# Dense feed-forward of a two-layer trunk: gate and up by seven half-size block products

## The chip, the cores and the metric

The kernel runs on one core of one Trainium2 chip. The metric is device time in microseconds (us), the median of several runs. Five engines work side by side and meet at semaphores: PE (TensorE) multiplies matrices, DVE (VectorE), ACT (ScalarE) and POOL (GpSimd) work on elements, SP (SyncE) issues the loads.

## What is computed

Two residual layers over 512 tokens of width 1024. The first has a mixer (gated convolution and a state-space scan) and then a dense SwiGLU; the second has differential attention and a mixture of 8 experts. The change concerns the dense SwiGLU, whose hidden width is 2816 = 22 tiles of 128:

```python
def swiglu(x, w_gate, w_up, w_down):
    return (jax.nn.silu(x @ w_gate) * (x @ w_up)) @ w_down

x = x + swiglu(rmsnorm(x, even_norm_ffn[i]), ffn_w_gate[i], ffn_w_up[i], ffn_w_down[i])
```

## The kernel before

Every product of float32 matrices is made of three passes. A matrix is split into a high part (rounded to TensorE's fp32r format) and a low part (the rest), and high x high, high x low and low x high are summed in PSUM. Activations are split once; weights are split as they arrive.

**Weight units.** `units` (L280 to L292) lists all weights of the trunk in the order of use, 512 KB each: `feature_unit` is 128 output features for all 1024 inputs, 8 blocks of 128 x 128; `token_unit` is 2 blocks of 128 inputs by 512 outputs. SP loads unit u into one of `RAW_SLOTS` = 4 slots of `raw` once POOL is through with unit u - 4 (`load`, L358). ACT rounds it into `w_hi` (`high_parts`, L993), one of `HL_SLOTS` = 4 slots, once TensorE has used unit u - 4 (`unit_used`). POOL subtracts, `w_lo = raw - w_hi` (`low_parts`, L1293, instruction L1305), and counts `lo_done`, for which TensorE waits in `begin_unit`. Each engine goes through its list in the order written by hand.

**Feed-forward.** The 22 hidden tiles come in two halves of 11 (`HALF_FT`), each followed by its part of the down projection (`token_out`, L430), which is added to the residual stream. A hidden tile n is two units, gate and up. `feature_out` (L419) makes one: 24 matmuls with 128 x 128 of weights held still and 512 tokens moving, into one PSUM bank:

```python
for k in range(KD):
    wh, wl = w_hi[:, s, k * P:(k + 1) * P], w_lo[:, s, k * P:(k + 1) * P]
    pe.matmul(ps[:, bank, :], wh, xh[:, k, :], start=(k == 0), stop=False)
    pe.matmul(ps[:, bank, :], wh, xl[:, k, :], start=False, stop=False)
    last = pe.matmul(ps[:, bank, :], wl, xh[:, k, :], start=False, stop=(k == KD - 1))
```

The first two tiles are made by `first_features` (L505) in two token halves of 256, because tokens 256 to 511 are still being normalized and turned then. Around a tile, ACT takes silu of the gate (L1151), DVE multiplies by the up bank (L1699, `ff_val`), ACT rounds the result (L1156, `ff_hi`), and POOL subtracts (L1381, `ff_lo`). `htmp` is a scratch tile of the normalization; `act_a_hi` and `act_a_lo` are the split activations, with features on partitions; `act_b_hi` and `act_b_lo` are free in this stage.

Of the kernel before, what the change touches and what calls it, by code (L numbers as in the profile page):

```python
# [16 lines left out]
F32 = mybir.dt.float32  # L17
# [4 lines left out]
ALU = mybir.AluOpType  # L22
# [64 lines left out]
FF_HALF = 2 * HALF_FT + 2 * HALF_UNITS  # L87
U_QKV = U_FF + 2 * FF_HALF
# [17 lines left out]
def build_trunk(nc, t, h_slots):  # L106
# [68 lines left out]

    q_tok, o = place("q_tok", [P, NT, D], F32, scratch)
# [105 lines left out]
    units = [feature_unit(w_in, COL_XBC + P * f) for f in range(XBC_TILES)]  # L282
    units += [token_unit(w_in, 2 * k, COL_Z + 512 * g) for g in range(2) for k in range(4)]
    units += [feature_unit(w_in, c + P * a) for a in range(KD) for c in (COL_CG, COL_HV, 0)]
    units += [token_unit(w_out, 2 * k, 512 * g) for g in range(2) for k in range(8)]
    for half in range(2):
        units += [feature_unit(w, P * f) for f in range(half * HALF_FT, (half + 1) * HALF_FT)
                  for w in (w_gate, w_up)]
        units += [token_unit(w_down, half * HALF_FT + 2 * k, 512 * g, min(2, HALF_FT - 2 * k))
                  for g in range(2) for k in range(HALF_UNITS)]  # L290
    units += [token_unit(w_qkv, 2 * k, 512 * g) for g in range(6) for k in range(4)]
    units += [token_unit(w_o, 2 * k, 512 * g) for g in range(2) for k in range(4)]  # L292
    assert len(units) == N_UNITS

    def size(u):
        return units[u][1][0] * units[u][1][1]
# [49 lines left out]
    def _(sp):  # L346
# [11 lines left out]
        def load(u):  # L358
            src, (k, n) = units[u]
            if u >= RAW_SLOTS:  # L360
                sp.wait_ge(lo_done, u - RAW_SLOTS + 1)
            sp.dma_start(raw[:, u % RAW_SLOTS, 0:k * n].rearrange("p (k n) -> p k n", k=k),
                         src).then_inc(unit_in[u % RAW_SLOTS], 16)
# [6 lines left out]
        for u in range(N_UNITS):  # L370
# [31 lines left out]
            if u == U_FF + 2 * FF_HALF - 6:  # L402
# [12 lines left out]
    def _(pe):  # L415
# [3 lines left out]
        def feature_out(u, bank, xh, xl):  # L419
# [8 lines left out]
            last.then_inc(unit_used, 1)  # L428

# [393 lines left out]
        for half in range(2):  # L823
            u0 = U_FF + half * FF_HALF
            if half:
                pe.wait_ge(acc_evac, 12)
            else:
                first_features(2, u0, lambda i: pe.wait_ge(acc_evac, 5 + i))
            for f in range(0 if half else 2, HALF_FT):
                n = half * HALF_FT + f  # L830
                pe.wait_ge(ff_mul, n - 1)
                feature_out(u0 + 2 * f, HID_BANK[half] + 2 * (n % 2), act_a_hi, act_a_lo)
                feature_out(u0 + 2 * f + 1, HID_BANK[half] + 2 * (n % 2) + 1, act_a_hi, act_a_lo)
            if half:
                pe.wait_ge(acc_evac, 16)
# [154 lines left out]
    def _(act):  # L990
        made = [0]

        def high_parts(upto):  # L993

            while made[0] <= min(upto, N_UNITS - 1):
                u = made[0]
                act.wait_ge(unit_in[u % RAW_SLOTS], 16 * (u // RAW_SLOTS + 1))
                if u >= HL_SLOTS:
                    act.wait_ge(unit_used, u - HL_SLOTS + 1)
                act.activation(w_hi[:, u % HL_SLOTS, 0:size(u)], raw[:, u % RAW_SLOTS, 0:size(u)],  # L1000
                               ACT.Copy).then_inc(hi_done, 1)
# [142 lines left out]
        for half in range(2):  # L1144
            u0 = U_FF + half * FF_HALF
            for f in range(HALF_FT):
                n = half * HALF_FT + f
                after(u0 + 2 * f)
                if n >= 2:
                    act.wait_ge(ff_mul, n - 1)  # L1150
                act.activation(ff_gate[:, n % 2, :], ps[:, HID_BANK[half] + 2 * (n % 2), :], ACT.Silu).then_inc(ff_silu, 1)  # L1151
                high_parts(u0 + 2 * f + 1 + AHEAD)
                act.wait_ge(ff_mul, n + 1)
                if half and f == 0:
                    act.wait_ge(unit_used, u0)
                act.activation(ff_hi[:, f, :], ff_val[:, n % 2, :], ACT.Copy).then_inc(ff_hi_done, 1)  # L1156
            high_parts(min(u0 + FF_HALF - 1 + AHEAD, U_QKV - 1))

# [251 lines left out]
    def _(dve):  # L1410
# [280 lines left out]
        for half in range(2):  # L1691
            u0 = U_FF + half * FF_HALF
            for f in range(HALF_FT):
# [3 lines left out]
                if n >= 2:  # L1697
                    dve.wait_ge(ff_lo_done, n - 1)
# [1289 lines left out]
```

## Time and profile before

| | |
|---|---|
| median of 3 runs | 1919.18 us (1919.08 to 1919.76) |
| the profiled execution, first to last instruction | 1917.3 us |
| TensorE busy | 1898.1 us, 99% of the span |
| DVE, ACT, POOL busy | 806.7, 717.9, 550.5 us |
| mean granted TensorE clock | 0.999 of full |
| feed-forward, gate and up of the first tile to the down projection's end | about 369 to 731 us |

The profile is of one execution; its span leaves out the start and the end of the program, and the median lies 1.9 us above it. Times within it count from the span's start. Matmuls overlap, so the step from one start to the next is what a matmul costs, and not its recorded duration. A DVE, ACT or POOL instruction's duration includes whatever it waited for after it was issued.

### The profile page before, as it was taken

Reading aid. Unit: us, or ns where it says so; the run is one execution under the profiler, and the core shown is the slowest. Engines: PE = TensorE matmul, PEld = TensorE weight load, DVE = VectorE, ACT = ScalarE, POOL = GpSimd, SP = SyncE. Lnnn points to the kernel's source line nnn. Section 1 sums busy time; section 2 is a strip of 40 time slices with the busy share of each in tenths; the row PEclk is TensorE's granted clock in tenths of the full one; section 3 lists DMA queues with packets and bytes.
Section 4 is the critical chain, followed back from the end, with each engine's and each line's share of the span. In section 5 each row is a group of like instructions: output and inputs, shape, how many; then the busy total and the mean of one; then the engine's idle time right before and its main releaser. Section 6 shows DMA issues by size and latency. Waiting matters only on the chain.

```text
span 1917.3 us, 29421 instructions
## 1 busy us (share of the span) xinstructions
PE 1898.1 (99%) x11978; PEld 1641.2 (86%) x11978; DVE 806.7 (42%) x1240; ACT 717.9 (37%) x1124; POOL 550.5 (29%) x332
## 2 busy tenths in 40 slices
PE   9999999999999999999999999999999999999998
PEld 7888788888888887877679999999999877888886
DVE  6465552200000006866741110100101776999996
ACT  5332232332222224367640001000000655878785
POOL 4466664365445544432321002010010100200000
PEclk9999999999999999999999999999999999999999
DMA  9523223233233332311119989888888787999993
GB/s 351 177 77 99 67 99 99 77 110 99 91 107 88 94 112 77 100 47 43 56 34 399 372 311 341 290 296 300 304 300 305 273 284 264 411 407 391 371 396 145
DMA packets 283561, 396.21 MB, mean 207 GB/s; under 512 B 12736, under 2 KB 190912, under 8 KB 283424
## 3 DMA queue, kind: packets, MB, share of 16 engines
q1 hardware_dynamic: 279488, 381.67, 56.7%
q0 software_dynamic: 3936, 12.62, 1.7%
q8 instruction: 97, 1.59, 0.3%
q14 instruction: 40, 0.33, 0.1%
HBM read 374.48 MB, written 21.08 MB: 206 GB/s over the span
## 4 chain that ended last, share of the span: by engine, by line
PE 96%; ACT 1%; DVE 1%; issue 1%; DMA 0%; DVEq 0%; POOL 0%; ACTq 0%; POOLq 0%; SPq 0%
PE ps L2200 17%; PE ps L2207 8%; PE ps L2264 6%; PE ps L2266 6%; PE ps L2265 6%; PE ps L425 6%; PE ps L427 6%; PE ps L426 6%; PE ps L443 3%; PE ps L445 3%; PE ps L444 3%; PE ps L572 2%; PE ps L574 2%; PE ps L573 2%; PE ps L462 1%; PE ps L460 1%
## 5 line engine op out<-in xcount | busy, mean ns | idle before, releaser
L1305 POOL TENSOR_TENSOR w_lo<-raw,w_hi 128x1024 fp32r<-128x1024 f32 (+2 forms) x193 | 386.9, 2021 | 346.9 <-ACT w_hi L1000 346.8
L2051 DVE TENSOR_TENSOR s_lo<-s_raw,s_hi 128x1024 fp32r<-128x1024 f32 x264 | 318.7, 1246 | 43.8 <-ACT s_hi L2461 36.3
L2461 ACT ACTIVATE s_hi<-s_raw 128x1024 fp32r<-128x1024 f32 x264 | 272.9, 1060 | 70.1 <-PE ps L2266 46.3
L1000 ACT ACTIVATE w_hi<-raw 128x1024 fp32r<-128x1024 f32 x158 | 163.4, 1043 | 188.0 <-PE ps L445 115.6
L2803 DVE TENSOR_TENSOR hid<-ps,silu_g 128x160 f32<-128x160 f32 x88 | 28.6, 325 | 409.9 <-ACT silu_g L2421 409.8
L425 PE MATMUL ps<-act_a_hi,w_hi 128*128 128x512 f32 x512 | 199.6, 390 | 0.0
L426 PE MATMUL ps<-act_a_lo,w_hi 128*128 128x512 f32 x512 | 199.3, 389 | 0.0
L427 PE MATMUL ps<-act_a_hi,w_lo 128*128 128x512 f32 x512 | 199.2, 389 | 0.0
L2584 POOL TENSOR_TENSOR sum_rows<-sum_rows,y_rows_sb 128x1024 f32<-128x1024 f32 (+1 forms) x12 | 28.6, 2380 | 580.1 <-ACT y_rows_sb L2426 320.4
L2421 ACT ACTIVATE silu_g<-ps 128x160 f32<-128x160 f32 x88 | 26.8, 304 | 447.6 <-PE ps L2200 447.6
L2200 PE MATMUL ps<-xT,w_gate 128*128 128x132 f32 x1408 | 172.9, 276 | 0.4 <-DMA w_up<-in_moe_w_up 0.4
L2200 PE MATMUL ps<-xT,w_up 128*128 128x132 f32 x1408 | 172.8, 276 | 0.0
L2200 PEld LDWEIGHTS ps<-xT,w_gate 128*128 128x128 f32 x1408 | 165.2, 190 | 0.6 <-issue 0.6
L2207 PE MATMUL ps<-hid,w_down 128*128 128x132 f32 x1408 | 165.4, 276 | 0.0
L2200 PEld LDWEIGHTS ps<-xT,w_up 128*128 128x128 f32 x1408 | 165.2, 190 | 0.0
L2207 PEld LDWEIGHTS ps<-hid,w_down 128*128 128x128 f32 x1408 | 161.5, 190 | 0.2
L2264 PE MATMUL ps<-s_hi,s_x_hi 128*128 128x512 f32 (+1 forms) x384 | 145.5, 379 | 0.0
L2266 PE MATMUL ps<-s_hi,s_x_lo 128*128 128x512 f32 (+1 forms) x384 | 142.9, 372 | 0.0
L2265 PE MATMUL ps<-s_lo,s_x_hi 128*128 128x512 f32 (+1 forms) x384 | 142.7, 372 | 0.0
L425 PEld LDWEIGHTS ps<-act_a_hi,w_hi 128*128 128x128 f32 x512 | 96.1, 188 | 22.3 <-issue 2.4
L427 PEld LDWEIGHTS ps<-act_a_hi,w_lo 128*128 128x128 f32 x512 | 96.1, 188 | 20.2
L426 PEld LDWEIGHTS ps<-act_a_lo,w_hi 128*128 128x128 f32 x512 | 96.1, 188 | 19.9
(464 smaller groups left out, 3158.4 us busy)
## 6 DMA issues: line engine op xcount, KB each, us to landing
w_gate<-in_moe_w_gate SPq DMA_DIRECT2D x44, 1024.0 KB, 5.3
w_up<-in_moe_w_up SPq DMA_DIRECT2D x44, 1024.0 KB, 8.5
w_down<-in_moe_w_down SPq DMA_DIRECT2D x44, 1024.0 KB, 10.5
s_raw<-in_moe_w_gate SPq DMA_DIRECT2D x44, 1024.0 KB, 8.3
s_raw<-in_moe_w_up SPq DMA_DIRECT2D x44, 1024.0 KB, 8.3
s_raw<-in_moe_w_down SPq DMA_DIRECT2D x44, 1024.0 KB, 8.0
raw<-in_even_w_in SPq DMA_DIRECT2D x42, 512.0 KB, 3.8
raw<-in_attn_w_qkv SPq DMA_DIRECT2D x24, 512.0 KB, 3.7
```

The lines of the kernel that those rows point to most:

```text
L425: pe.matmul(ps[:, bank, :], wh, xh[:, k, :], start=(k == 0), stop=False)
L426: pe.matmul(ps[:, bank, :], wh, xl[:, k, :], start=False, stop=False)
L427: last = pe.matmul(ps[:, bank, :], wl, xh[:, k, :], start=False, stop=(k == KD - 1))
L1000: act.activation(w_hi[:, u % HL_SLOTS, 0:size(u)], raw[:, u % RAW_SLOTS, 0:size(u)], ACT.Copy).then_inc(hi_done, 1)
L1305: ins = pool.tensor_tensor(w_lo[:, u % HL_SLOTS, cut], raw[:, u % RAW_SLOTS, cut], flat(w_hi[:, u % HL_SLOTS, cut]), ALU.subtract)
L2051: return eng.tensor_tensor(s_lo[u % S_HL][:], s_raw[u // 2 % S_RAW][:, u % 2, :], s_hi[u % S_HL][:].bitcast(F32), ALU.subtract)
L2200: mm = pe.matmul(ps[:, bank, i * CAP:i * CAP + width], w_slots[s][i][:, k, c:c + P], xT[:, k, 0:width], start=(k == 0), stop=(k == KD - 1))
L2207: mm = pe.matmul(ps[:, d // 3, (d % 3) * CAP:(d % 3) * CAP + width], w_slots[s][2][:, f % 2, d * P:(d + 1) * P], hid[:, f, 0:width], start ...
L2264: pe.matmul(out, sh, wh, start=first, stop=False, skip_group_check=True)
L2265: pe.matmul(out, sh, wl, start=False, stop=False, skip_group_check=True)
L2266: return pe.matmul(out, sl, wh, start=False, stop=last, skip_group_check=True)
L2461: act.activation(s_hi[u % S_HL][:], s_raw[q % S_RAW][:, u % 2, :], ACT.Copy).then_inc(s_high, 1)
```

## The change

Tiles 0 and 1 stay as they were. For each of the other 20 tiles the kernel takes gate and up as one product of blocks. The inputs (k) are cut in two halves of 512, the tokens in two halves of 256, and the outputs are gate and up, so that each of four results (gate or up, tokens low or high) was the sum of two block products, eight in all. A scheme of the Strassen-Winograd kind makes the four results of seven block products, on sums of blocks:

- **Weights.** DVE makes four sums of weight blocks for each tile, 512 wide: t1 and t4 in `w_sums_b`, t2 and t3 in `w_sums_a`, which is `htmp` (`weight_sums`). A tile is now four units (`paired`): the gate as loaded, `w_sums_a`, `w_sums_b`, and half of the up as loaded. ACT rounds and POOL subtracts 3.5 x 1024 columns a tile where it was 2 x 1024. Loads are a list of their own (`loads`, `freed_by`).
- **Activations.** Four sums of activation blocks, 1024 wide, are made once: `h_feat` is the unsplit activation (ACT copies it from PSUM for tokens 256 to 511, POOL adds high and low parts for tokens 0 to 255), DVE makes the sums, ACT rounds them to `act_b_hi`, DVE subtracts to `act_b_lo`.
- **Products.** `paired_out` makes the seven products, 12 matmuls of 256 columns each. Partial results are kept in SBUF: ACT copies the first (`part_1`); DVE adds (`part_16`, `part_167`, and four more sums). `part_kept` and `part_read` tell TensorE that a bank may be written again.
- **Hidden tile.** Silu is taken in two halves; the second waits for `late_gate`. The product of gate and up now has both inputs in SBUF. The low part `ff_lo` moves from POOL to DVE (`low_hidden`).

```diff
+        def paired_out(n):
+            u0, b, m = pair_unit(n), pair_bank(n), n - PLAIN_F
...
+            def product(bank, u, at, source, first):
+                s = u % HL_SLOTS
+                for k in range(4):
+                    xh, xl = source(k)
+                    c = at + k * P
+                    wh, wl = w_hi[:, s, c:c + P], w_lo[:, s, c:c + P]
+                    pe.matmul(ps[:, bank, 0:256], wh, xh, start=(first and k == 0), stop=False, skip_group_check=True)
+                    pe.matmul(ps[:, bank, 0:256], wh, xl, start=False, stop=False, skip_group_check=True)
+                    last = pe.matmul(ps[:, bank, 0:256], wl, xh, start=False, stop=(k == 3), skip_group_check=True)
+                return last
+
+            first_pair = n == PLAIN_F
+            begin_unit(u0)
+            if n != PLAIN_F + 1:
+                pe.wait_ge(ff_mul, n - 1)
+            product(b, u0, 0, from_tile(0, 0), True).then_inc(part_done, 1)
+            begin_unit(u0 + 1)
...
+            product(b + 1, u0 + 1, 0, from_sum(1), True).then_inc(part_done, 1)
+            pe.wait_ge(part_kept, m + 1)
+            product(b, u0, 512, from_tile(4, 0), False).then_inc(unit_used, 1)
...
+            product(b + 2, u0 + 1, 512, from_sum(2), True).then_inc(unit_used, 1)
+            begin_unit(u0 + 2)
...
+            product(b + 3, u0 + 2, 0, from_sum(0), True).then_inc(part_done, 1)
+            pe.wait_ge(part_read, 2 * m + 1)
+            product(b + 2, u0 + 2, 512, from_tile(4, 256), False).then_inc(unit_used, 1)
+            begin_unit(u0 + 3)
...
+            pe.wait_ge(part_read, 2 * m + 2)
+            product(b + 3, u0 + 3, 0, from_sum(3), False).then_inc(unit_used, 1)
...
+        for n in range(PLAIN_F, FT):
+            u0, b, m = pair_unit(n), pair_bank(n), n - PLAIN_F
+            act.wait_ge(part_done, 3 * m + 1)
...
+            act.activation(part_1[:], ps[:, b, 0:256], ACT.Copy).then_inc(part_kept, 1)
+            if n != HALF_FT:
+                high_hidden(n - 1)
+            act.wait_ge(unit_used, u0 + 1)
+            act.activation(ff_gate[:, n % 2, 0:256], ps[:, b, 0:256], ACT.Silu).then_inc(ff_silu, 1)
+            high_parts(u0 + 5)
+            act.wait_ge(late_gate, m + 1)
+            act.activation(ff_gate[:, n % 2, 256:512], part_1[:], ACT.Silu).then_inc(ff_silu, 1)
+            high_parts(u0 + 7)
...
+        low_parts(U_FF + 1)
+        for tt in (0, 1):
+            cut = slice(tt * P, (tt + 1) * P)
+            pool.wait_ge(lo_ev, 8 + 2 * tt + 2)
+            pool.tensor_tensor(h_feat[:, :, cut], flat(act_a_hi[:, :, cut]), flat(act_a_lo[:, :, cut]), ALU.add
+                               ).then_inc(h_kept, 1)
         low_parts(U_WO - 1)
...
+        def weight_sums(n):
...
+            if m:
+                dve.wait_ge(lo_done, pair_unit(n - 1) + 3)
+            dve.tensor_tensor(t1, b12, b11, ALU.subtract)
+            dve.tensor_tensor(t3, b22, b12, ALU.subtract)
+            dve.drain()
+            dve.tensor_tensor(t2, b22, t1, ALU.subtract)
+            dve.drain().then_inc(w_sums_made, 1)
+            dve.tensor_tensor(t4, b21, t2, ALU.subtract).then_inc(w_sums_made, 1)
...
+            dve.tensor_tensor(part_16[:], ps[:, b + 1, 0:256], part_1[:], ALU.add)
+            if n + 1 < FT and n + 1 != HALF_FT:
+                weight_sums(n + 1)
+            dve.wait_ge(unit_used, u0 + 2)
+            dve.drain()
+            dve.tensor_tensor(part_167[:], ps[:, b + 2, 0:256], part_16[:], ALU.add).then_inc(part_read, 1)
```

How DVE's list changes: before, these two rows were all that DVE did for the 11 tiles of the first half (`ps` is PSUM, `x9` counts repeats):

```order
L1699 TENSOR_TENSOR ff_val_88<-ps,ff_gate_87 128x512 [waits ff_silu,unit_used] x2
L1699 TENSOR_TENSOR ff_val_88<-ps,ff_gate_87 128x512 [waits ff_lo_done,ff_silu,unit_used] x9
```

Now DVE has these rows for one paired tile, here tile 2, with the weight sums of tile 3 in it (the line numbers are of the changed file):

```order
L1896 TENSOR_TENSOR part_16_91<-ps,part_1_90 128x256 [waits part_kept,part_done]
L1853 TENSOR_TENSOR w_sums_b_89<-raw_54 128x512 [waits lo_done,unit_in1,unit_in0]
L1854 TENSOR_TENSOR htmp_58<-raw_54 128x512
L1856 TENSOR_TENSOR htmp_58<-raw_54,w_sums_b_89 128x512
L1858 TENSOR_TENSOR w_sums_b_89<-raw_54,htmp_58 128x512
L1901 TENSOR_TENSOR part_167_92<-ps,part_16_91 128x256 [waits unit_used]
L1904 TENSOR_TENSOR ff_val_88<-ps,part_167_92 128x256 [waits part_done]
L1906 TENSOR_TENSOR part_1_90<-ps,part_16_91 128x256 [waits unit_used]
L1908 TENSOR_TENSOR ff_val_88<-ps,part_16_91 128x256 [waits unit_used]
L1911 TENSOR_TENSOR ff_val_88<-ff_val_88,ff_gate_87 128x512 [waits ff_silu]
L1868 TENSOR_TENSOR ff_lo_86<-ff_val_88,ff_hi_85 128x512 [waits ff_hi_done]
```

One instruction a tile has become eleven; six of them, L1853 to L1858, L1911 and L1868, read nothing from `ps`. The sum `part_167`, for which TensorE's sixth product waits, stands behind the four weight sums of the next tile.

POOL's list where the feed-forward begins; before (the 18 are units up to the fifth of the feed-forward):

```order
L1305 TENSOR_TENSOR w_lo_56<-raw_54,w_hi_55 128x1024 [waits hi_done] x18
L1381 TENSOR_TENSOR ff_lo_86<-ff_val_88,ff_hi_85 128x512 [waits ff_hi_done]
L1305 TENSOR_TENSOR w_lo_56<-raw_54,w_hi_55 128x1024 [waits hi_done] x2
```

and now (the 15 are units up to its second):

```order
L1458 TENSOR_TENSOR w_lo_56<-raw_54,w_hi_55 128x1024 [waits hi_done] x15
L1531 TENSOR_TENSOR h_feat_93<-act_a_hi_50,act_a_lo_51 128x8x128 [waits lo_ev] x2
L1458 TENSOR_TENSOR w_lo_56<-raw_54,w_hi_55 128x1024 [waits hi_done] x3
L1458 TENSOR_TENSOR w_lo_56<-htmp_58,w_hi_55 128x1024 [waits hi_done]
L1458 TENSOR_TENSOR w_lo_56<-w_sums_b_89,w_hi_55 128x1024 [waits hi_done]
L1458 TENSOR_TENSOR w_lo_56<-raw_54,w_hi_55 128x512 [waits hi_done]
```

The two additions stand ahead of the third unit of the feed-forward, and each paired tile has three subtractions of 1024 and one of 512 in a row.

## Rows read from the trace of the kernel before

**Rows 1.** the page: engines, the chain that ended last, weight loads.
```profile
PE 1898.1 (99%) x11978; PEld 1641.2 (86%) x11978; DVE 806.7 (42%) x1240; ACT 717.9 (37%) x1124; POOL 550.5 (29%) x332
...
PE 96%; ACT 1%; DVE 1%; issue 1%; DMA 0%; DVEq 0%; POOL 0%; ACTq 0%; POOLq 0%; SPq 0%
...
L425 PEld LDWEIGHTS ps<-act_a_hi,w_hi 128*128 128x128 f32 x512 | 96.1, 188 | 22.3 <-issue 2.4
```

**Rows 2.** busy time by stretch, feed-forward; behind POOL the granted clock, DMA share, GB/s.
```profile
395.00:440.00 45.00, 45.00 (x200) 37.28 (x199) 2.77 (x4) 13.60 (x18) 25.79 (x14) 1.00 0.39 115
```

**Rows 3.** timeline of TensorE, 512 columns: start us, duration us, engine, line, operation.
```profile
393.58 0.40 PE L425 MATMUL ps<-act_a_hi,w_hi 128*128 128x512 f32 x1
...
404.49 0.39 PE L425 MATMUL ps<-act_a_hi,w_hi 128*128 128x512 f32 x1
...
415.37 0.39 PE L425 MATMUL ps<-act_a_hi,w_hi 128*128 128x512 f32 x1
```

**Rows 4.** the list of waits, TensorE's longest: us in total, times, longest us.
```profile
PE ps L668 <- POOLq L1317: 2.3, 1, 2.3
```

**Rows 5.** timeline of TensorE, 256 columns.
```profile
376.23 0.36 PE L518 MATMUL ps<-act_a_hi,w_hi 128*128 128x256 f32 x1
...
382.06 0.28 PE L518 MATMUL ps<-act_a_hi,w_hi 128*128 128x256 f32 x1
...
393.22 0.28 PE L518 MATMUL ps<-act_a_hi,w_hi 128*128 128x256 f32 x1
```

**Rows 6.** timeline of ACT beside the third tile.
```profile
399.74 1.05 ACT L1000 ACTIVATE w_hi<-raw 128x1024 fp32r<-128x1024 f32 x1
405.42 0.63 ACT L1156 ACTIVATE ff_hi<-ff_val 128x512 fp32r<-128x512 f32 x1 [4.62 <-DVE ff_val L1699]
```

**Rows 7.** timeline of POOL: four units, the third of the feed-forward, the third tile.
```profile
300.64 9.46 POOL L1305 TENSOR_TENSOR w_lo<-raw,w_hi 128x1024 fp32r<-128x1024 f32 x4 [16.32 <-ACT w_hi L1000]
...
370.98 3.40 POOL L1305 TENSOR_TENSOR w_lo<-raw,w_hi 128x1024 fp32r<-128x1024 f32 x1
...
400.87 2.39 POOL L1305 TENSOR_TENSOR w_lo<-raw,w_hi 128x1024 fp32r<-128x1024 f32 x1 [1.79 <-ACT w_hi L1000]
406.12 1.29 POOL L1381 TENSOR_TENSOR ff_lo<-ff_val,ff_hi 128x512 fp32r<-128x512 f32 x1 [2.86 <-ACT ff_hi L1156]
```

**Rows 8.** timeline of DVE beside the third tile.
```profile
404.69 0.69 DVE L1699 TENSOR_TENSOR ff_val<-ps,ff_gate 128x512 f32<-128x512 f32 x1 [10.21 <-PE ps L427]
```

**Rows 9.** instruction groups by form, 256 wide, on DVE and on ACT: busy us, mean ns.
```profile
L1746 DVE TENSOR_TENSOR htmp<-ps,rot_s 128x256 f32<-128x256 f32 x16 | 6.6, 413 | 0.0
...
L1203 ACT ACTIVATE probs<-ps,soft 128x256 f32<-128x256 f32 x16 | 7.4, 464 | 1.9 <-DVE soft L1764 1.9
```

**Rows 10.** DMA issues: count, KB each, us to landing.
```profile
raw<-in_ffn_w_gate SPq DMA_DIRECT2D x22, 512.0 KB, 3.7
```

**Rows 11.** timeline of DVE where POOL is busy too.
```profile
133.82 2.10 DVE L1611 SCALAR_TENSOR_TENSOR mix<-mix,cbm 128x512 f32<-128x512 f32 x1
135.85 1.52 DVE L1611 SCALAR_TENSOR_TENSOR mix<-mix,cbm 128x512 f32<-128x512 f32 x1
...
756.39 0.68 DVE L1745 TENSOR_TENSOR htmp<-ps,rot_c 128x512 f32<-128x512 f32 x1
...
757.83 0.69 DVE L1751 TENSOR_TENSOR htmp<-htmp 128x512 f32<-128x512 f32 x1
...
758.71 2.63 DVE L1755 TENSOR_TENSOR q_tok<-htmp,head_ss 128x512 f32<-128x512 f32 x1
```

**Rows 12.** timeline of POOL in the same stretches, one instruction a row.
```profile
133.47 1.91 POOL L1333 TENSOR_TENSOR xdt<-xs,dts 128x1024 f32<-128x1024 f32 x1
135.33 1.50 POOL L1346 TENSOR_TENSOR spans<-act_b_lo,dts 128x512 fp32r<-128x512 f32 x1
...
755.35 2.42 POOL L1305 TENSOR_TENSOR w_lo<-raw,w_hi 128x1024 fp32r<-128x1024 f32 x1 [13.09 <-ACT w_hi L1000]
757.84 2.94 POOL L1305 TENSOR_TENSOR w_lo<-raw,w_hi 128x1024 fp32r<-128x1024 f32 x1
```

More of the change, by code:

```diff
@@ L291, in build_trunk, with plain, paired @@
-    units += [token_unit(w_qkv, 2 * k, 512 * g) for g in range(6) for k in range(4)]
-    units += [token_unit(w_o, 2 * k, 512 * g) for g in range(2) for k in range(4)]
+    loads, units, freed_by = [], [], []
+    def plain(parts):
+        for src, shape in parts:
+            units.append(("raw", len(loads), 0, shape[0] * shape[1]))
+            freed_by.append(len(units))
+            loads.append((src, shape))
+    def paired(gate, up):
+        r, u = len(loads), len(units)
+        loads.extend((gate, up))
+        freed_by.extend((u + 3, u + 4))
+        units.extend((("raw", r, 0, UNIT), ("sums_a", 0, 0, UNIT), ("sums_b", 0, 0, UNIT), ("raw", r + 1, UNIT // 2, UNIT // 2)))
@@ L293, in build_trunk, with whole, wait_whole @@
+    plain(token_unit(w_qkv, 2 * k, 512 * g) for g in range(6) for k in range(4))
+    plain(token_unit(w_o, 2 * k, 512 * g) for g in range(2) for k in range(4))
     assert len(units) == N_UNITS
     def size(u):
-        return units[u][1][0] * units[u][1][1]
+        return units[u][3]
+    def whole(u):
+        home, r, at, n = units[u]
+        tile = {"raw": raw[:, r % RAW_SLOTS, :], "sums_a": w_sums_a, "sums_b": w_sums_b}[home]
+        return tile[:, at:at + n]
+    def wait_whole(eng, u):
+        home, r, at, n = units[u]
+        if home == "raw":
+            eng.wait_ge(unit_in[r % RAW_SLOTS], 16 * (r // RAW_SLOTS + 1))
+        else:
+            half = u >= U_PAIRS[1]
+            m = (u - U_PAIRS[half]) // PAIR_UNITS + (HALF_FT - PLAIN_F if half else 0)
+            eng.wait_ge(w_sums_made, 2 * m + (1 if home == "sums_a" else 2))
@@ L369, in _ @@
         zero_blocks = range(0, h_slots.shape[0], P)
-        for u in range(N_UNITS):
+        for u in range(len(loads)):
             load(u)
@@ L401, in _ @@
                 load_gain(3)
[L402 removed]
+            if u == units[U_QKV - 6][1]:
                 sp.wait_ge(ff_lo_done, FT)
@@ L827, in _ @@
             else:
[L828 to L835, printed above, removed]
+                first_features(2, U_FF, lambda i: pe.wait_ge(acc_evac, 5 + i))
+            for n in range(HALF_FT if half else PLAIN_F, HALF_FT * (half + 1)):
+                if n == HALF_FT + 1:
+                    pe.wait_ge(acc_evac, 16)
+                paired_out(n)
             def hidden_tiles(i, tt):
@@ L1143, in _ @@
         norm_by_tile(1, 2, U_FF, lambda tt: act.wait_ge(acc_evac, 5 + tt))
[L1144 to L1157, printed above, removed]
+        for tt in (2, 3):
+            for half in range(2):
+                act.wait_ge(lo_ev, 8 + 2 * tt + half + 1)
+                act.activation(h_feat[:, 4 * half:4 * half + 4, tt * P:(tt + 1) * P],
+                               ps[:, TURN_BANK[2] + (2 * tt + half) % 4, :].rearrange("p (a b) -> p a b", a=4), ACT.Copy
+                               ).then_inc(h_kept, 1)
```

203 lines of the change are left out of this document (150 added, 53 removed).

## The prediction, made before the changed kernel was run

> **What bounds the kernel now.** I read the page first: TensorE is busy 99% of the span, and it makes up 96% of the chain that ended last [rows 1]. So a saving has to shorten TensorE's own work, and whatever makes it wait is paid in full. Then the busy times by stretch, for the feed-forward [rows 2]: in 45 us TensorE has no gap at full granted clock (1.00, the 2.4 GHz level), POOL is busy 25.8 us and DVE 2.8. POOL, not DVE, is the engine with work there. Then the timelines. A hidden tile n (gate and up) begins every 10.9 us [rows 3]: 48 matmuls of 512 columns at 0.2267 us. The list of waits has nothing over 2.3 us on TensorE [rows 4].
>
> **The matmuls.** Matmuls of 256 columns already run in the first two tiles: from 382.06 to 393.22 there are 93 starts, 0.120 us each [rows 5]. A paired tile has 7 products of 12, 84 x 0.120 = 10.08 us, against 10.88. That is 0.80 less, 16.1 us for 20 tiles: less than the eighth that the count of columns promises (1.36 a tile), since a matmul costs some 13 ns beside its columns at both sizes. This is all the change can gain.
>
> **What it adds to the others, per paired tile.** ACT rounds four weight units (three of 1024, one of 512) where it had two, 1.05 us for 1024 [rows 6]. POOL subtracts the same four: 3 x 2.36 + 1.25 = 8.33 us, from four in a row in 9.46 us, single ones being recorded at 2.39 and 1.29 [rows 7]; its 1.29 us low part of the hidden tile goes to DVE. DVE had one instruction of 0.69 us [rows 8]; now it has four weight sums of 512, five sums of 256 out of PSUM at 0.41 [rows 9], the product and the low part: some 5.5 us back to back. Loads are as many as before, two of 512 KB a tile, each landed 3.7 us after its issue [rows 10]; their raw slots come free with POOL's third and fourth unit, and they land some 5 us ahead of their weight sums. I cost them at nothing; if POOL's units slip over 5 us more, they are next.
>
> **The port between DVE and POOL.** This decides. At 757.83 DVE begins a tensor_tensor with both inputs in SBUF, and the POOL unit that begins at 757.84 takes 2.94 us instead of 2.39. At 758.71 DVE asks for another one: it takes 2.63 instead of 0.69 and ends 0.56 us after that POOL unit [rows 11, 12]. Between engines that both have work they alternate, one instruction each: at 133.82 two DVE instructions in a row take 2.10 and 1.52 us, each ending 0.54 after a POOL instruction [rows 11, 12]. With one input in PSUM there is no such wait: 0.68 us at 756.39, in the middle of a POOL unit of 2.42 [rows 11, 12]. Of DVE's new instructions, six have both inputs in SBUF: the four weight sums, the product of ff_val and ff_gate, and the low part. Before, no DVE instruction of these tiles did. The port then needs 8.33 + 6 x 0.54 = 11.6 us a tile, already over 10.88.
>
> **The loop that sets the pace.** TensorE's sixth product waits for part_read, which DVE gives after the next tile's weight sums. Without the port: the second product ends 3.1 us into the tile; product and low part of the tile before are done by 3.2; part_16 at 3.6, four weight sums with two drains by 6.3, part_167 at 6.8. It is needed at 7.2 less 0.24 (a weight load of 0.19 [rows 1] and a hop of 0.05, estimated): 0.15 us to spare, where one port wait is up to 2.4. With the port, from the start of a sixth product: it and its tail 1.64; DVE part_1 0.42 (2.1); ACT's late silu, 256 wide, 0.3 (2.4; the nearest row, a 256 wide exponential, has 0.46 [rows 9]); ACT rounds the third unit of the next tile (3.5); POOL subtracts it, and the product waits behind it (5.9); product 0.69 (6.5); ACT rounds the hidden tile 0.63 (7.2); DVE's low part waits behind POOL's fourth unit and ends at 8.3; part_16 and the first weight sum (9.1); POOL has meanwhile taken its turn with the first unit of the tile after, and the second weight sum waits for it, to 12.1; third and fourth with their drains 13.7; part_167 14.2; TensorE goes on at **14.4**. That is 10.08 of work and a stall of 4.3 us ahead of each sixth product. Every step is a row or a sum of rows; the ends are small: hops of 0.02 or 0.08, POOL 5% faster or slower and a hop to TensorE of 0.1 or 0.35 move it from 13.8 to 14.7.
>
> It holds for the tiles that have a late tile before them and a weight sum behind: not for n = 10 and 21, which make no sums for a next tile, nor for n = 11, which begins after the down projection with all its units ready. Tile 2 comes as late, since its low parts wait on the sums of activations. 17 x (14.4 - 10.88) = +59.8 us; 3 x (10.08 - 10.88) = -2.4.
>
> **The first two tiles.** POOL now adds two tiles of h_feat ahead of its third weight unit. Before, that unit ran from 370.98 to 374.38 [rows 7], and TensorE took it at 376.23 [rows 5]. The adds are 2.4 us each (the size of a unit; at least 1.9, as the 1024 wide row at 133.47 [rows 12]), so the unit ends at 379.1: **+3.0** (+2 to +3.5). The other sums of activations on DVE and ACT, about 5 us and 4 us, lie beside the 11.5 us of the second token half. Behind the last tile nothing moves.
>
> **Sum**: +59.8 - 2.4 + 3.0 = +60.4. On the profiled span of 1917.3 that is 1977.7; the runs' median is 1.9 above that span, so **1979.6 us**, said as 1980. A measurement of this kernel can tell about 0.2%, 3.8 us, from no change.
>
> **Rivals.**
> - *A clock that falls.* Before, TensorE never waits over 2.3 us [rows 4] and its clock reads 1.00. Now it would stand for 4.3 us of every 14.4. If the clock goes to its 1.2 GHz level there, the sixth product takes up to 1.43 us more, and it is in the loop (the seventh is mostly not: the product waits for POOL anyway): 17 x 1.43 = +24, 2004 us. No row speaks for or against, as no such gap is in the trace; the stretch at work between two gaps, 10 us, speaks against a lasting fall. Chance 0.17. The Trainium skill (TensorE: Matmul & The Clock Gate, HAM oscillation) says that a kernel with waits between bursts falls to half rate at each wait and has to earn the clock again; by that rule the time would be this rival's, and no run here shows it yet.
> - *The port packs well.* If DVE and POOL fill it without holes, a tile costs the port's 11.6 us: 17 x 0.7 - 2.4 + 3.0 = +12.5, about 1932 us. For it: the port's sum is a floor. Against it: the loop above is a chain of waits in a fixed order, with the port empty in two places of it (while DVE sums out of PSUM and while ACT rounds). It decides if the third unit reaches POOL before DVE's last sum. Anything between this and the forecast is possible. Chance 0.10. The Trainium skill (SBUF — State Buffer, SBUF: two separate sides) has the pair of ports locked by whoever starts first for the whole instruction, not shared by bandwidth; sharing would bring the time toward this rival, and the rows at 757.83 and 758.71 side with the lock.
> - *Faster after all.* If two SBUF inputs cost DVE no wait on these tiles, or under 0.15 us, the tile is 10.08: -16.1 + 3.0 = -13.1, 1906 us. Its place is the sixth product's wait, its price 0.80 us a tile gained. Against it stand six port waits a tile. Chance 0.05.
> - *That the change doesn't do what it says* can be left out: the listing of its instructions has 84 matmuls of 256 columns for a paired tile.
>
> **How the numbers follow.** Forecast 0.68, with 1965 to 1992 as its own range. The clock 0.17, packing 0.10, faster 0.05. The range must leave out no more than 2 in 10: from 1945 (packing in part) to 2010 (the clock). Faster 0.05, within 0.2% 0.01, slower 0.94.
>
> **What would show it.** Right: in the timeline, tiles 3 to 9 and 13 to 20 begin 14.4 us apart, 10 and 11 10.1 apart; TensorE waits 4 us for DVE's part_167, 17 times; DVE's second weight sum is recorded at 2.5 to 3 us, the product at over 2.5; POOL's units stay under 3. Weight sums of 0.69 us beside a busy POOL would make the loop wrong; matmuls of 0.21 us behind the stall would show the clock; tiles at 11.6 the packing. If the first weight sum waits instead of the second, the time is the same within 0.3 us a tile.

## The result, and the profile after

The changed kernel takes **1990.38 us** (median of 4 runs, 1990.19 to 1990.86) against 1919.22 of the kernel before (4 runs): a ratio of 1.0372, with a 95% interval of 1.0357 to 1.0387. It is slower, as forecast, and the time lies 10.4 us above the 1980 of the prediction, inside its range. The profiled execution's span went from 1917.3 to 1988.5 us, +71.2.

The page of the changed kernel: engines, granted clock of TensorE by slice, chain that ended last.

```profile
PE 1916.1 (96%) x12698; PEld 1693.1 (85%) x12698; DVE 1004.8 (51%) x1450; ACT 768.2 (39%) x1212; POOL 621.9 (31%) x352
...
PEclk9999999988999889999999999999999999999999
...
PE 86%; DVE 7%; ACT 2%; POOL 1%; DVEq 1%; issue 1%; DMA 0%; ACTq 0%; POOLq 0%; SPq 0%
```

TensorE went from 96% of the chain [rows 1] to 86%, and DVE from 1% to 7%. TensorE's busy time did not fall but rose by 18 us, although the paired tiles have fewer columns. Slower matmuls are in it: the granted clock falls below nine tenths only in slices of the feed-forward, and by their starts the slow matmuls of the paired tiles take 26 us more than they would at full pace. The list of waits of the changed kernel (us in total, times, longest) names the new ones:

```profile
PE ps L519 <- DVE part L1901: 50.9, 17, 5.2
PE ps L639 <- POOL w_lo L1458: 2.6, 1, 2.6
```

L1901 makes `part_167`, and L519 begins the sixth product. The second row is the prologue, which is what I call the stretch ahead of the first paired tile. By stretch, in the changed kernel (busy us of PE, PEld, DVE, ACT, POOL, then granted clock, DMA share, GB/s):

```profile
395.00:440.00 45.00, 34.95 (x255) 34.34 (x253) 34.00 (x34) 18.88 (x28) 27.66 (x13) 0.85 0.28 83
```

Against [rows 2], DVE is busy 34.0 us where it had 2.8, POOL hardly more (27.7 against 25.8), and the clock is 0.85 in place of 1.00. More than a third of DVE's 34 us is waiting inside instructions: in this stretch and with the times that each form takes alone (0.42, 0.69 and, for 1024 columns, 1.23 us in e7), its instructions would take some 22 us (an estimate). One tile shows the waits. DVE in the changed kernel (start, us, line, operands):

```profile
431.78 1.79 DVE L1911 TENSOR_TENSOR ff_val<-ff_val,ff_gate 128x512 f32<-128x512 f32 x1
434.27 1.01 DVE L1868 TENSOR_TENSOR ff_lo<-ff_val,ff_hi 128x512 fp32r<-128x512 f32 x1 [0.70 <-ACT ff_hi L1278]
...
435.54 0.68 DVE L1853 TENSOR_TENSOR w_sums_b<-raw 128x512 f32<-128x512 f32 x1
436.13 0.68 DVE L1854 TENSOR_TENSOR htmp<-raw 128x512 f32<-128x512 f32 x1
436.89 0.69 DVE L1856 TENSOR_TENSOR htmp<-raw,w_sums_b 128x512 f32<-128x512 f32 x1
437.70 2.66 DVE L1858 TENSOR_TENSOR w_sums_b<-raw,htmp 128x512 f32<-128x512 f32 x1
440.45 0.42 DVE L1901 TENSOR_TENSOR part<-ps,part 128x256 f32<-128x256 f32 x1
```

and POOL beside it:

```profile
430.62 2.40 POOL L1458 TENSOR_TENSOR w_lo<-w_sums_b,w_hi 128x1024 fp32r<-128x1024 f32 x1 [2.68 <-ACT w_hi L1117]
432.98 1.75 POOL L1458 TENSOR_TENSOR w_lo<-raw,w_hi 128x512 fp32r<-128x512 f32 x1
437.04 2.76 POOL L1458 TENSOR_TENSOR w_lo<-raw,w_hi 128x1024 fp32r<-128x1024 f32 x1 [2.32 <-ACT w_hi L1117]
439.76 2.82 POOL L1458 TENSOR_TENSOR w_lo<-htmp,w_hi 128x1024 fp32r<-128x1024 f32 x1
```

The product ends 0.55 us behind POOL's unit (433.57 against 433.02), the low part 0.55 behind the next (435.28 against 434.73), the fourth weight sum 0.56 behind the one after (440.36 against 439.80): the pattern of [rows 11, 12], three times in a tile. TensorE in the changed kernel, around its stalls:

```profile
425.75 0.58 PE L519 MATMUL ps<-act_a_hi,w_hi 128*128 128x256 f32 x1 [3.31 <-DVE part L1901]
...
426.56 0.41 PE L519 MATMUL ps<-act_a_hi,w_hi 128*128 128x256 f32 x1
426.78 0.41 PE L520 MATMUL ps<-act_a_lo,w_hi 128*128 128x256 f32 x1
...
438.20 0.28 PE L521 MATMUL ps<-act_b_hi,w_lo 128*128 128x256 f32 x1
440.93 0.39 PE L519 MATMUL ps<-act_a_hi,w_hi 128*128 128x256 f32 x1 [2.45 <-DVE part L1901]
```

Behind this stall the matmuls start 0.21 us apart where they need 0.12: the lower of the two clock levels, for one product or two. The fall doesn't always come at once. In tile 6 the sixth product begins at 470.88 at the full pace and slows down near its end; ten of the seventeen tiles have such a delay:

```profile
471.94 0.28 PE L521 MATMUL ps<-act_a_hi,w_lo 128*128 128x256 f32 x1
472.06 0.32 PE L519 MATMUL ps<-act_a_hi,w_hi 128*128 128x256 f32 x1
472.18 0.41 PE L520 MATMUL ps<-act_a_lo,w_hi 128*128 128x256 f32 x1
472.39 0.42 PE L521 MATMUL ps<-act_a_hi,w_lo 128*128 128x256 f32 x1
```

Behind the stall of tile 12, 3.6 us long, no matmul is slow. From all starts in this trace: tiles 2 to 9 and 12 to 20 take between 13.6 and 17.1 us, 14.89 on the mean, against 10.88 before; 10, 11 and 21 take 10.1 to 10.3. The first pair starts at 397.96 in place of 393.58 [rows 3]. So 17 x (14.89 - 10.88) = +68.2, three tiles -2.1, prologue +4.4: +70.5 of the span's +71.2.

### The profile page after: what moved, and what is told of

Same layout as the page of the kernel before. It is cut to its first block, busy times and chain, and to the rows that moved or that the text cites. A ratio compares the mean times of both kernels' runs of the same rounds, so it can differ in the third digit from the quotient of the medians.

```text
span 1988.5 us, 31362 instructions
## 1 busy us (share of the span) xinstructions
PE 1916.1 (96%) x12698; PEld 1693.1 (85%) x12698; DVE 1004.8 (51%) x1450; ACT 768.2 (39%) x1212; POOL 621.9 (31%) x352
## 4 chain that ended last, share of the span: by engine, by line
PE 86%; DVE 7%; ACT 2%; POOL 1%; DVEq 1%; issue 1%; DMA 0%; ACTq 0%; POOLq 0%; SPq 0%
PE ps L2413 16%; PE ps L2420 8%; PE ps L2477 6%; PE ps L2479 6%; PE ps L2478 6%; PE ps L564 3%; PE ps L565 3%; PE ps L566 3%; PE ps L495 2%; PE ps L496 2%; PE ps L497 2%; PE ps L693 2%; PE ps L519 2%; PE ps L695 2%; PE ps L694 2%; PE ps L521 2%
## 5 line engine op out<-in xcount | busy, mean ns | idle before, releaser
L1458 POOL TENSOR_TENSOR w_lo<-raw,w_hi 128x1024 fp32r<-128x1024 f32 (+2 forms) x193 | 377.6, 1974 | 337.2 <-ACT w_hi L1117 337.0
L1117 ACT ACTIVATE w_hi<-raw 128x1024 fp32r<-128x1024 f32 (+1 forms) x158 | 154.9, 990 | 185.4 <-PE ps L566 103.4
L519 PE MATMUL ps<-act_a_hi,w_hi 128*128 128x256 f32 x240 | 76.0, 317 | 50.9 <-DVE part L1901 50.9
L519 PEld LDWEIGHTS ps<-act_a_hi,w_hi 128*128 128x128 f32 x240 | 51.7, 216 | 54.4 <-DVE part L1901 54.3
L519 PE MATMUL ps<-act_b_hi,w_hi 128*128 128x256 f32 x320 | 97.6, 305 | 0.0
L520 PE MATMUL ps<-act_b_lo,w_hi 128*128 128x256 f32 x320 | 97.1, 303 | 0.0
L521 PE MATMUL ps<-act_b_hi,w_lo 128*128 128x256 f32 x320 | 96.7, 302 | 0.0
L2477 PEld LDWEIGHTS ps<-s_hi,s_x_hi 128*128 128x128 f32 x384 | 72.3, 188 | 14.1 <-issue 1.6
## 6 DMA issues: line engine op xcount, KB each, us to landing
w_down<-in_moe_w_down SPq DMA_DIRECT2D x44, 1024.0 KB, 10.3
```

Source lines behind the costliest of these rows:

```text
L519: pe.matmul(ps[:, bank, 0:256], wh, xh, start=(first and k == 0), stop=False, skip_group_check=True)
L520: pe.matmul(ps[:, bank, 0:256], wh, xl, start=False, stop=False, skip_group_check=True)
L521: last = pe.matmul(ps[:, bank, 0:256], wl, xh, start=False, stop=(k == 3), skip_group_check=True)
L1117: act.activation(w_hi[:, u % HL_SLOTS, 0:size(u)], whole(u), ACT.Copy).then_inc(hi_done, 1)
L1458: ins = pool.tensor_tensor(w_lo[:, u % HL_SLOTS, cut], whole(u)[:, cut], flat(w_hi[:, u % HL_SLOTS, cut]), ALU.subtract)
L2477: pe.matmul(out, sh, wh, start=first, stop=False, skip_group_check=True)
```

## The experiments

Runs that were made together share runs of the kernel before: its median is 1921.29 for e1 to e4, 1919.27 for e5 to e7, 1919.16 for e8 and e9. Ratios are to those.

**e1_no_port: is it the port?** For the tiles from 3 on (tile 11 left out), each weight sum reads a bank of PSUM that TensorE is through with in place of one of its two blocks, and the hidden product stays in PSUM, so no DVE instruction of the loop has two inputs in SBUF. ACT and POOL round and subtract the raw block for the two summed units. Instructions are as many. The weight sums and all that follows from them have other values; the experts then get other numbers of rows, so that the whole time (one run, 2613.48 us, span 2611.7) means nothing and only the feed-forward is read.

```diff
...
-            dve.tensor_tensor(t1, b12, b11, ALU.subtract)
...
+            there = ps[:, pair_bank(n - 1) + 1, :] if n not in (PLAIN_F, HALF_FT) else None
+            for out, one, two, then in ((t1, b12, b11, 0), (t3, b22, b12, 2), (t2, b22, t1, 3), (t4, b21, t2, 1)):
...
+                    ins = dve.tensor_tensor(out, there, two, ALU.subtract)
...
```

> DVE's instructions stay as many and as long, but none of the paired tiles' reads two inputs in SBUF: the weight sums read a PSUM bank in place of one block (so the sums are wrong, and the rounding takes the gate's block instead; all that follows is computed on wrong values), and the hidden product is held in PSUM. If waits for the port between DVE and POOL make the loop: tiles 3 to 9 and 13 to 20 begin 10.1 us apart instead of 14.8, TensorE's wait for part_167 is gone, the granted clock is 1.00, and the down projection ends about 80 us earlier. If it is DVE's own work and its order: tiles stay over 13 us and the wait stays. The expert layer gets other values and perhaps other routing, so only the stretch up to the down projection's end is compared.

Measured: every tile from 4 on takes 10.08 us (tile 3: 10.24), and only tile 2 waits for `part_167`. The window behind it, same columns as above:

```profile
440.00:480.00 40.00, 40.00 (x336) 40.00 (x335) 23.81 (x44) 20.30 (x32) 33.72 (x16) 1.00 0.36 103
```

The timeline of e1 shows DVE's hidden product, its low part and the first weight sum inside four POOL units in a row, which end at 429.19, and the second weight sum across their end, each at its own length:

```profile
420.71 8.48 POOL L1462 TENSOR_TENSOR w_lo<-raw,w_hi 128x1024 fp32r<-128x1024 f32 x4 [2.85 <-ACT w_hi L1117]
```
```profile
425.57 0.70 DVE L1925 TENSOR_TENSOR ps<-ps,ff_gate 128x512 f32<-128x512 f32 x1
427.41 0.69 DVE L1881 TENSOR_TENSOR ff_lo<-ps,ff_hi 128x512 fp32r<-128x512 f32 x1 [1.14 <-ACT ff_hi L1281]
...
428.35 0.68 DVE L1862 TENSOR_TENSOR w_sums_b<-ps,raw 128x512 f32<-128x512 f32 x1
428.94 0.68 DVE L1862 TENSOR_TENSOR htmp<-ps,raw 128x512 f32<-128x512 f32 x1
```

Same engines, same chain of waits, same count of work; with one input moved to PSUM the loss is gone, all of it. It is the port, and the gain of 0.80 us a tile was real. The last paired matmul starts at 666.0, 75 us ahead of the changed kernel.

**e2_val_in_psum: two port instructions fewer.** The hidden product is held in PSUM (L1911 and L1868 then have one input there); the weight sums stay.

```diff
...
+                dve.tensor_tensor(ff_lo[:, f, :], ps[:, pair_bank(n) + 1, :],
+                                  flat(ff_hi[:, f, :]), ALU.subtract).then_inc(ff_lo_done, 1)
...
-            dve.tensor_tensor(ff_val[:, n % 2, :], ff_val[:, n % 2, :], ff_gate[:, n % 2, :], ALU.mult).then_inc(ff_mul, 1)
+            dve.tensor_tensor(ps[:, b + 1, :], ps[:, b + 1, :], ff_gate[:, n % 2, :], ALU.mult).then_inc(ff_mul, 1)
...
```

> Only the hidden product and its low part lose their second SBUF input (the values are held in a PSUM bank that TensorE has finished with); the weight sums keep theirs. Waiting for whole POOL instructions: the product no longer waits for a POOL unit, tiles 12.8 to 13.1 us apart, 1960 us (1955 to 1967). If only the sum of port times counted (0.54 us for each of the two): 1972. If the clock alone made the difference: no change, 1990.

1958.19 us (1955.13 to 1960.16), 1.0189 (1.0172 to 1.0206): nearly half of the loss comes back. The total is as expected, the tiles are not: they do not take 13 us each but, from tile 5 on and with few exceptions, in turn 14.2 and 10.1. In the long ones the fourth weight sum takes 2.65 us, in the short ones 0.69. My reading, which no run tests, is that the wait in one tile shifts DVE against POOL so that the sums of the next are clear of its units. The long tiles hold slow matmuls too: 14.2 us is 10.1 of work, a stall 2.6 longer than a step, and 1.5 of lower clock.

```profile
PE ps L519 <- DVE part L1909: 30.8, 12, 5.2
```

**e3_pool_in_pieces: the same instructions on DVE, POOL's in pieces.** POOL's subtractions in the feed-forward are cut to 256 columns.

```diff
-                step = 256 if u >= U_QKV + 20 else 1024
+                step = 256 if u >= U_QKV + 20 or U_PAIRS[0] <= u < U_DOWN[0] or U_PAIRS[1] <= u < U_DOWN[1] else 1024
```

> POOL's subtractions of the paired tiles in pieces of 256 columns instead of 1024, everything else as in the change. If DVE waits for the POOL instruction that holds the port, whatever its length, it now waits 0.66 us at most: tiles about 12.8 to 13.3 us apart, 1963 us (1956 to 1972), though POOL is busy longer (0.66 us a piece, 9.2 us a tile for 8.3). If it is POOL's total work that counts: slower, 2003.

1965.76 us (1964.99 to 1967.04), 1.023 (1.0213 to 1.0248). A DVE instruction now waits for one piece only. DVE in e3, a second and a third weight sum:

```profile
432.26 1.22 DVE L1854 TENSOR_TENSOR htmp<-raw 128x512 f32<-128x512 f32 x1
433.56 1.07 DVE L1856 TENSOR_TENSOR htmp<-raw,w_sums_b 128x512 f32<-128x512 f32 x1
```

So the waits have the length of POOL's instruction, not of its work; but now every sum pays some 0.4 us, where one in four paid 2.0. The four together still wait 1.7 us a tile; the hidden product, at 0.69 to 1.26 us in place of 1.77 to 2.92, gained more.

**e4_fill_the_stall: does the clock cost anything?** Twenty-two idle matmuls of 128 columns run in each stall, their output never read. They write a bank that DVE has read for the tile before, so TensorE first waits for that tile's product (`ff_mul`), which is done by then.

```diff
+            if n not in (HALF_FT - 1, HALF_FT, FT - 1):
+                pe.wait_ge(ff_mul, n)
+            for _ in range(0 if n in (HALF_FT - 1, HALF_FT, FT - 1) else 22):
+                pe.matmul(ps[:, pair_bank(n - 1) + 1, 0:P], ones[:], t_incl[:], start=True, stop=True, skip_group_check=True)
             pe.wait_ge(part_read, 2 * m + 1)
```

> 22 matmuls of 128 columns without use (some 2.2 us) between TensorE's fifth and sixth product, where it stands still for 2.4 to 4 us; no engine waits for them. If the fall of the clock costs what rows of the change show (sixth and seventh product at up to 0.229 us a matmul): granted clock back to 1.00, all matmuls at 0.120, tiles 14.4 us apart, 1983 us (1979 to 1986). If the slow matmuls lie beside DVE's and POOL's loop: clock back, time the same within 2 us.

1993.27 us (1992.6 to 1994.0), 1.0376 (1.0359 to 1.0394), no different from the changed kernel; clock 1.00, tiles of 14.99 (tile 2: 15.56). It looks as if the clock were free, but the trace says otherwise. TensorE in e4, where `part_167` had ended at 438.21:

```profile
434.27 5.08 PE L546 MATMUL ps<-t_incl,ones 128*128 128x128 f32 x44
439.10 0.36 PE L519 MATMUL ps<-act_a_hi,w_hi 128*128 128x256 f32 x1
```

An idle matmul shows as two records 0.112 us apart, so that the 22 last 5 us, where I had taken 2.2; together they outlast the stall: the sixth product begins 0.89 us behind `part_167`, where without them it follows 0.06 behind (440.93 after 440.87 in the changed kernel). That is 0.8 us a tile. This run fills too much and proves nothing; e8 does it again.

**e8_shorter_fill.** The same with 16.

```diff
-            for _ in range(0 if n in (HALF_FT - 1, HALF_FT, FT - 1) else 22):
+            for _ in range(0 if n in (HALF_FT - 1, HALF_FT, FT - 1) else 16):
```

> The same filling of the stall with 16 idle matmuls in place of 22. In the run with 22 the idle matmuls lasted from 434.27 to 439.35, while part_167 had ended at 438.21: the filling itself held the sixth product back by some 0.65 us, 17 times, so that run could not show what the lower clock costs. Sixteen take 3.6 us of a stall of 3.9 and end before part_167. If the lower clock behind a stall is on the path: tiles of 14.3 to 14.4 us where the changed kernel has 14.9 on the mean, 17 x 0.5 = 9 less, some 1981 us, ratio 1.0325 (1.031 to 1.034). If the lower clock costs nothing: tiles of 14.9, ratio 1.037 as the changed kernel.

**1977.38 us** (five runs 1976.49 to 1978.32; one more took 1995.32, at a mean granted clock of 0.947, for a reason that the record doesn't show), 1.032 (1.0291 to 1.0348), below the changed kernel's interval: the lower clock costs the changed kernel 13 us. The tiles take 14.17 us each, without spread but for tile 2 (15.56) and tile 12 (13.67), 14.22 on the mean. The twelve matmuls of the sixth product, from the first start to the first of the seventh, take 26.1 us over the 17 tiles, where the changed kernel has 37.1; these 11.0 us are nearly all of the 11.4 by which the 17 tiles differ. TensorE and DVE in e8:

```profile
435.68 3.74 PE L546 MATMUL ps<-t_incl,ones 128*128 128x128 f32 x32
439.67 0.39 PE L519 MATMUL ps<-act_a_hi,w_hi 128*128 128x256 f32 x1 [0.26 <-DVE part L1905]
```
```profile
429.18 2.92 DVE L1915 TENSOR_TENSOR ff_val<-ff_val,ff_gate 128x512 f32<-128x512 f32 x1
432.79 1.01 DVE L1872 TENSOR_TENSOR ff_lo<-ff_val,ff_hi 128x512 fp32r<-128x512 f32 x1 [0.70 <-ACT ff_hi L1282]
...
434.66 2.87 DVE L1858 TENSOR_TENSOR htmp<-raw 128x512 f32<-128x512 f32 x1
...
439.19 0.42 DVE L1905 TENSOR_TENSOR part<-ps,part 128x256 f32<-128x256 f32 x1
```

With the clock held this is the forecast's loop, step by step. The sixth product began at 425.49 (one tile before 439.67); from there the product ends at 6.6 (forecast 6.5), the low part at 8.3 (8.3), the second weight sum, which is the one that waits, at 12.0 (12.1), `part_167` at 14.1 (14.2).

**e5_h_feat_later: the prologue.** POOL adds h_feat behind the third and fourth weight unit, not ahead of them.

```diff
-        low_parts(U_FF + 1)
+        low_parts(U_FF + 3)
```

> Only the order of POOL in the first tiles: the two additions of h_feat behind the fourth weight unit instead of behind the second. TensorE's wait of 2.6 us for the third unit goes; if nothing else takes its place the time is 2.5 us less than that of the change (3.7% above the kernel before becomes 3.6%). If the sums of activations then come later and tile 2 waits for them, the gain is given back at tile 2, and the time is that of the change within 1 us.

1989.55 us (1987.34 to 1990.03), 1.0363 (1.0345 to 1.038). The 2.6 us wait at L639 is gone and the first pair starts at 394.70, 3.3 earlier; but tile 2 takes 19.53 in place of 17.13, with a wait that was not there:

```profile
PE ps L519 <- DVE ff_val L1863: 3.0, 1, 3.0
```

2.4 of 3.3 us are given back at once: the sums of activations come later, and with them tile 1's hidden product (L1863), which stands behind three of their low parts in DVE's list and for which tile 2's fourth product waits.

**e6_sums_after_parts: the order on DVE.** The next tile's weight sums go behind `part_167` and the second half of the values, so that nothing with two SBUF inputs stands ahead of what TensorE waits for.

```diff
-            if n + 1 < FT and n + 1 != HALF_FT:
-                weight_sums(n + 1)
             dve.wait_ge(unit_used, u0 + 2)
...
             dve.tensor_tensor(ff_val[:, n % 2, 256:512], ps[:, b + 3, 0:256], part_167[:], ALU.add).then_inc(part_read, 1)
+            if n + 1 < FT and n + 1 != HALF_FT:
+                weight_sums(n + 1)
```

> Only DVE's order: part_167 and the first half of ff_val ahead of the four weight sums of the next tile, so that TensorE's sixth and seventh product wait for no weight sum. If the waits for the port stand in a loop and not only in front of one product, the stall moves: TensorE then waits for the second unit of the next tile (rounded and subtracted late), tiles 12.7 us apart (12.3 to 13.5), about 35 us less than the change, 1.7 to 2.3% above the kernel before. If the sixth product's wait was all of it, tiles go to 10.1 us and the kernel is 0.3 to 0.5% faster than before.

1972.79 us (1972.27 to 1974.96), 1.0281 (1.0264 to 1.0298), outside the 1.7 to 2.3% that I expected. Tiles take 12.5 or 14.0, and the wait has another name; this is the list of waits of e6:

```profile
PE ps L519 <- POOL w_lo L1458: 39.3, 18, 2.3
```

The sixth product is free; the second now waits, for a unit that POOL can only make after the sums. The loop has closed through POOL. Order alone brings back a quarter of the loss (17.6 of 71.2 us) while six instructions a tile take the port. What I had missed is the clock again. All eighteen stalls are alike, 2.44 to 2.57 us from start to start, but behind thirteen of them matmuls are slow. By stretch, tile 8 and tile 9 of e6 (columns as above):

```profile
479.41:491.93 12.52, 10.34 (x86) 10.14 (x85) 9.35 (x12) 5.17 (x8) 9.27 (x4) 1.00 0.30 85
491.93:505.92 13.99, 11.82 (x86) 11.62 (x85) 9.33 (x12) 5.18 (x8) 9.23 (x4) 0.88 0.26 77
```

The tiles with the clock up are the 12.7 us that I expected; thirteen others cost 1.5 us more, some 19 us together, which is the miss.

**e7_less_port: both.** The hidden product is in PSUM as in e2. DVE itself subtracts one of the two summed units (1.23 us for 1024, where POOL needs 2.40), so that POOL has three turns at the port in a tile and DVE five. The four weight sums are spread: two ahead of `part_167`, the third behind the values, the fourth behind `part_1`; the low part of the hidden tile moves to the next tile's start, and POOL's h_feat adds as in e5.

```diff
+            if n != HALF_FT:
+                low_hidden(n - 1)
...
+            if more:
+                first_sums(n + 1)
...
+            if more:
+                third_sum(n + 1)
...
+            if more:
+                fourth_sum(n + 1)
+            if more:
+                own_low_part(n + 1)
```

> A version meant to beat both: the hidden product in PSUM (as in e2), DVE makes the low part of the second unit of 18 of the tiles in place of POOL (1.2 us on the port for 2.4), part_167 and the second half of the values ahead of the third and fourth weight sum, the low part of the hidden tile at the start of the next, and POOL's additions as in e5. The port is then taken 6.0 us by POOL and 2.1 + 1.2 us by DVE of 10.1. If the port's waits were the whole loss: tiles 10.2 to 10.5 us apart, 1910 us (1905 to 1916), faster than both. If a wait of another kind stands behind them, tiles over 11 us and slower than before.

**1910.79 us** (1909.41 to 1912.38), 0.9956 (0.9942 to 0.997): 0.4% faster than the kernel before, and faster than the changed one. Every paired tile from 3 on takes 10.08 us. DVE and POOL in one tile of e7:

```profile
430.38 1.23 DVE L1889 TENSOR_TENSOR w_lo<-htmp,w_hi 128x1024 fp32r<-128x1024 f32 x1
...
434.33 1.56 DVE L1868 TENSOR_TENSOR w_sums_b<-raw 128x512 f32<-128x512 f32 x1
435.81 0.68 DVE L1869 TENSOR_TENSOR htmp<-raw 128x512 f32<-128x512 f32 x1
...
438.42 0.88 DVE L1874 TENSOR_TENSOR htmp<-raw,w_sums_b 128x512 f32<-128x512 f32 x1
...
439.76 0.68 DVE L1879 TENSOR_TENSOR w_sums_b<-raw,htmp 128x512 f32<-128x512 f32 x1
```
```profile
431.68 2.40 POOL L1474 TENSOR_TENSOR w_lo<-w_sums_b,w_hi 128x1024 fp32r<-128x1024 f32 x1 [3.01 <-ACT w_hi L1126]
434.04 1.29 POOL L1474 TENSOR_TENSOR w_lo<-raw,w_hi 128x512 fp32r<-128x512 f32 x1
436.35 2.40 POOL L1474 TENSOR_TENSOR w_lo<-raw,w_hi 128x1024 fp32r<-128x1024 f32 x1 [1.02 <-ACT w_hi L1126]
```

Two of DVE's four sums fall into POOL's pauses, and its subtraction of 1024 with them; the longest port wait is 0.88 us (the first sum), and it lies beside TensorE's work. Four things were changed at once here; which of them were needed, no run tells. Tile 2 still takes 16.47, against 10.88 of a tile before.

**e9_tile_2_order: tile 2 of e7.** The second plain tile's product goes ahead of two low parts of the sums of activations.

```diff
+        weigh_plain(1)
         low_sum(0, 3)
-        low_hidden(0)
-        weigh_plain(1)
         low_sum(3, 4)
+        low_hidden(0)
```

> e7_less_port with the second plain tile's product moved ahead of the third and fourth low part of the sums of activations, and the first hidden tile's low part behind them. In e7 tile 2 takes 16.47 us in place of 10.08, and its fourth product waits 3.1 us for that product, which DVE has behind three low parts (7.32 us at 391.70). If that order is what tile 2 loses: the wait of 3.1 us goes, some of it comes back as a wait for the third low part or for part_167, tile 2 takes 12.5 to 14 us, total 1907 to 1909, ratio 0.994 (0.993 to 0.995). If the port beside POOL's four units is what it loses, the wait only moves to a later product and the time stays at 1910.8.

1911.69 us (1910.76 to 1912.29), 0.9961 (0.9949 to 0.9974): no gain. The wait of 3.1 us for the product went and came back as one for `part_167`; from the list of waits of e9:

```profile
PE ps L528 <- DVE part L1937: 5.5, 1, 5.5
```

Tile 2 takes 17.37. That its low parts and POOL's four units want the port in the same 10 us, whatever the order, is my reading; what would free it was not tried.

## Why the prediction was right, and where it was off

- **What bounds it.** Right: whatever makes TensorE wait was paid in full.
- **The matmuls.** Right: 10.08 us a tile where nothing waits (e1, e7; 10.07 in tile 11 of the changed kernel).
- **The port decides.** Right, and shown by e1: the same work with one input in PSUM loses nothing. The Trainium skill (SBUF — State Buffer, SBUF: two separate sides) says that the lock holds for the whole instruction; e3 agrees, since the waits shrank from 2.0 to 0.4 us with the length of POOL's instruction. The rival of a well packed port, 11.6 a tile, did not come.
- **The loop.** Right in its steps and its 14.4 us, at full clock: e8 has 14.17. In the changed kernel the mean is 14.89, so the term came out at +68.2 where the sum had +59.8, and TensorE's wait for `part_167` is 3.0 us on the mean of the list, not 4. The step that failed is the one ahead of it, that the clock stays up. With slow matmuls in the sixth product, DVE's `part_1` comes later and all behind it slides against POOL. So the third or the fourth weight sum waits in 13 of the 17 tiles, where the prediction named the second, which is the one in e8 (tiles 3 to 9 and 13 to 20); and the product is mostly recorded at 1.8 to 2.9 us, where it had over 2.5.
- **The clock.** It was a rival with a chance of 0.17 and 24 us; it is true for 13 of them (1990.4 less 1977.4). I had let "the stretch at work between two gaps, 10 us" speak against a lasting fall. It does not last, but behind 16 of the 17 stalls, which are 2.4 to 5.5 us from start to start, some matmuls ran at the lower level, 0.21 us apart. No row of before could show it: TensorE waited 2.3 us at most there [rows 4], at a clock of 1.00. The Trainium skill's rule (TensorE: Matmul & The Clock Gate, HAM oscillation), a fall to half rate at each wait, was the better guide, but the trace differs from it in two places: tile 12 has no slow matmul, and in ten of the other sixteen the first 3 to 11 matmuls behind the stall still ran at the full pace. That is also why the price was smaller than 24. The rival took all twelve matmuls of the sixth product as slow, at 0.240; the slow ones are at 0.213, and in those ten tiles the clock came down only in the course of the twelve. The twelve starts of a sixth product lie between 0.129 and 0.229 us apart on the mean, and it lasts 0.65 us longer than in e8 on the mean, not 1.43.
- **The first two tiles.** +4.4 measured against +3.0. The wait for POOL's third unit, 2.6 us in the list, is the step I had costed: TensorE takes the unit at 379.10 in place of 376.23, +2.9. The other 1.5 us are the clock again: behind that wait sixteen matmuls ran at 0.213 us (at 381.11 and 381.32, for two). Tile 2 was forecast as a tile like the others and took 17.13; 15.56 with the clock held (e8).
- **Costs put at nothing.** Right: neither loads nor ACT appear among the new waits of TensorE, and the three terms make up all but 0.7 of the 71.2 us.

The sum made again for e8, where the clock is out of the paired tiles: the seventeen tiles +56.8, three -2.4, prologue +5.2, together +59.6; the span has +59.2, the forecast +60.4. That the two are so near is in part luck: the loop came out 3.0 us under its term and the prologue 2.2 over, 0.9 of which e8 had lost before its feed-forward began.

## What to carry to other kernels

When work is moved to DVE beside a busy POOL, count the DVE instructions with both inputs in SBUF, not their microseconds: each can wait for a whole POOL instruction, and one input left in PSUM takes that wait away. Then draw the loop of waits once round; shortening one part of it (e6) moves the wait, and only fewer turns at the port together with another order (e7) brought the saved matmuls out as time. And where a change puts a wait of a few microseconds ahead of TensorE's work, price the slower matmuls behind it too.

## What the hardware showed that was not expected

- Behind 16 of 17 stalls of 2.4 to 5.5 us the granted clock fell: the sixth or the seventh product runs at up to 0.229 us a matmul of 256 columns, against 0.120. The length of the stall alone doesn't decide it: of e6's eighteen stalls, all near 2.45 us, five have no slow matmul behind them, and neither has one of 3.6 us in the changed kernel. Idle matmuls in the stall kept it up (e8, clock 0.998) and made the kernel 13 us faster, though they compute nothing; 22 in place of 16 took all of it back (e4).
- With a lower demand for the port the tiles don't get evenly faster but mostly take 14.2 and 10.1 us in turn (e2).
- A DVE subtraction of 1024 columns with both inputs in SBUF takes 1.23 us against POOL's 2.40 for the same (e7).
